# Cached attention of a two-layer hybrid decoder: queries on rows, three column groups, a product scan, and one chain of four-page units over all samples

## What is computed

```python
def stick_breaking(q, k, v, q_pos, k_pos):
    z = jnp.einsum('bqhd,bkhd->bhqk', q, k).astype(jnp.float32) * HEAD_DIM ** -0.5
    causal = (k_pos[None, :] < q_pos[:, None])[None, None]
    log_beta = jax.nn.log_sigmoid(z)
    log_keep = jnp.where(causal, jax.nn.log_sigmoid(-z), 0.0)
    after = lax.cumsum(log_keep, axis=3, reverse=True) - log_keep
    a = jnp.where(causal, jnp.exp(log_beta + after), 0.0)
    return jnp.einsum('bhqk,bkhd->bqhd', a.astype(v.dtype), v)

    logits = jnp.einsum('bqgrd,bqkgd->bqgrk', qg, kg).astype(jnp.float32) * HEAD_DIM ** -0.5
    logits = jnp.where(valid[:, :, None, None, :], logits, -jnp.inf)
    p = jax.nn.softmax(logits, axis=-1)
    o = jnp.einsum('bqgrk,bqkgd->bqgrd', p.astype(v.dtype), vg)
```

## Time and profile before

| | |
|---|---|
| median of 3 runs | 5645.08 us (5630.95 to 5647.56) |
| profiled execution | 5633.87 us, span 5632.3 us |
| samples' attention, layer 0 | 2113 to 2583 us of the span |
| samples' attention, layer 1 | 4908 to 5385 us |
| granted PE clock, mean of the span | 0.933 |

### The profile page before, as it was taken

One profiled execution on the slowest core, in us unless ns is written; L12 is line 12 of the kernel. 1 busy time (PEld: TensorE's weight loads), 2 busy tenths in 40 slices (PEclk: granted clock), 3 DMA queues, 4 the chain that ended last, 5 costly groups with the idle time before them and its releaser, 6 DMA issues.

```text
span 5632.3 us, 72888 instructions
## 1 busy us (share of the span) xinstructions
...
## 2 busy tenths in 40 slices
...
GB/s 61 32 9 51 58 21 53 53 61 98 60 46 22 18 69 133 183 138 144 106 38 30 11 58 48 21 59 62 50 105 48 48 20 24 90 145 151 168 97 89
DMA packets 344766, 390.79 MB, mean 69 GB/s; under 512 B 102775, under 2 KB 266706, under 8 KB 340978
## 3 DMA queue, kind: packets, MB, share of 16 engines
...
## 4 chain that ended last, share of the span: by engine, by line
PE 78%; DVE 7%; issue 5%; ACT 4%; SPq 2%; POOL 1%; DMA 1%; ACTq 1%; POOLq 0%; DVEq 0%
PE banks L801 17%; PE banks L804 13%; PE banks L1748 8%; PE banks L312 5%; PE banks L1509 4%; PE banks L1077 4%; PE banks L1109 4%; PE banks L1094 4%; DVE arena L402 3%; PE banks L1534 3%; PE banks L1501 3%; PE banks L1292 3%; PE banks L1307 2%; PE banks L1282 2%; ACT arena L1321 1%
## 5 line engine op out<-in xcount | busy, mean ns | idle before, releaser
L903 DVE TENSOR_SCALAR_CACHE_REDUCE arena<-arena 128x384 uint8<-128x384 f32 (+14 forms) x960 | 1405.1, 1533 | 7.2 <-DVE arena L941 0.9
L801 PE MATMUL banks<-arena 128*128 128x512 f32 x2176 | 937.4, 592 | 0.0
L804 PE MATMUL banks<-arena 128*128 128x384 f32 (+3 forms) x2336 | 720.3, 464 | 3.0 <-POOLq L147 3.0
L801 PEld LDWEIGHTS banks<-arena 128*128 128x128 f32 x2176 | 409.9, 189 | 523.2 <-issue 523.2
L1193 DVE TENSOR_TENSOR_SCAN arena<-arena 128x129 f32<-128x129 f32 (+3 forms) x480 | 525.7, 1139 | 142.5 <-ACT arena L1121 121.6
L1337 POOL TENSOR_SCALAR arena<-arena 128x128 f32<-128x128 f32 (+15 forms) x192 | 577.8, 3021 | 138.4 <-DVE arena L1367 138.4
L804 PEld LDWEIGHTS banks<-arena 128*128 128x128 f32 (+1 forms) x2336 | 417.5, 182 | 269.3 <-issue 62.9
L1748 PE MATMUL banks<-arena 128*128 128x512 f32 (+1 forms) x1088 | 471.3, 596 | 13.0 <-SPq L147 13.0
L1356 DVE CUSTOM_DVE_ANT_0 arena<-banks,arena 128x512 f32<-128x512 f32 (+3 forms) x480 | 274.1, 608 | 333.8 <-PE banks L1282 313.4
L336 PE MATMUL banks<-arena 64*128 64x512 f32 (+3 forms) x1216 | 321.0, 627 | 136.8 <-ACT arena L384 134.5
L402 DVE SCALAR_TENSOR_TENSOR arena<-arena 128x512 f32<-128x512 f32 (+3 forms) x532 | 393.1, 739 | 56.3 <-ACT arena L384 0.7
...
## 6 DMA issues: line engine op xcount, KB each, us to landing
arena<-in_cache_sb_kv SPq DMA_DIRECT2D x256, 384.0 KB
arena<-in_cache_dsa_kv SPq DMA_DIRECT2D x256, 128.0 KB
...
```

Source lines behind the costliest of these rows:

```text
L801: m = nc.tensor.matmul(bank[i % 4][:, :], W2[c % 2][:, k, j * P:(j + 1) * P], xT[:, k, t * FREE:(t + 1) * FREE], start=(k == 0), stop=(k = ...
L804: m = nc.tensor.matmul(bank[i % 4][0:rows_of(t), 0:WD[name]], xT[:, k, t * P:t * P + rows_of(t)], W2[c % 2][:, k, 0:WD[name]], start=(k == ...
L903: nc.vector.tensor_scalar(out[0:r, 0:v.shape[-1]], v, thr[0:r, t:t + 1], 0.0, ALU.is_ge, ALU.add, accum_out=cnt[0:r, t:t + 1]).then_inc(s_ ...
```

## The change

`sattn_*` is written anew. The logits of both mixers now stand with queries on partitions and keys in columns. The work of all 8 samples is one straight chain of 40 **units**, five to a sample: the 8 new keys (c = 0), then four chunks of four pages, last pages first. Page buffers are per chunk (8 for stick, 10 for sparse). In step s of the chain PE does `logits(s-1)`, `keys(s)`, `weights(s-3)` and `values(s-4)`.

- Per unit the stick logits are three matmuls of 512 columns, one for each head pair, whose outputs lie at partitions 0, 32 and 64 of one bank (32, 32 and 16 query rows); the sparse logits are one of 48 rows.
- ACT takes the sigmoid of minus z, DVE a product scan from the last key backwards, carried from unit to unit, POOL the difference of neighbours, which is the weight. Exp, Ln, softplus, the 16-step sum and the constant matrices are gone.
- PE transposes the weights (80 rows stick, 48 rows sparse, the sparse ones five units later, after the softmax of the whole sample), DVE copies both to SBUF, PE applies the values in the same three column groups.
- ACT loads the sigmoid table before the stage and changes to the Exp table and back once per sample. It also issues half of the sparse page loads.
- The bias is stored as one row per sample, head and query (384 rows, 48 DMAs at the start of the stick stage where there were 8) and loaded by two DMAs per sample. Query rows of all samples are loaded once. Results are stored once, by 12 DMAs after the chain, and waited for at t = 2 of the output stage.
- Small set-up constants change (`negtri`, `negones`, `newmask`, `newbias` go, `octets`, `notcausal` come).

The diff, cut to what the steps speak of:

```diff
-    SBD = nc.dram_tensor("sample_bias", (NS, NKEY), F32).ap()
+    SBD = nc.dram_tensor("sample_bias", (NB * HDSA * NQ, NKEY), F32).ap()
...
-                sp.dma_start(SBD[b * NQ:(b + 1) * NQ, :], scs[a:a + 2 * NQ - 1:2, :]).then_inc(s_bs, 16)
+                for h in range(HDSA):
+                    r = (b * HDSA + h) * NQ
+                    sp.dma_start(SBD[r:r + NQ, :], scs[a:a + 2 * NQ - 1:2, :]).then_inc(s_bs, 16)
...
+                    sp.wait_ge(s_az0, at(s_az0, l + 1))
+                    load_queries(sp, l)
+                    load_first_pages(sp, l)
...
+            nc.gpsimd.memset(alg_1[:, 0:2 * NB * P], 0.0).then_inc(s_az0, 1)
...
+        ACH, APC, NAU = 5, 4, 5 * NB
+        SROWS, DROWS, CW4 = 80, HDSA * NQ, APC * P
+        NAV = NAU + ACH
...
+        QROWS = (32, 32, 16)
...
+        def chunk(n):
+
+            b, c = unit(n)
+            return 4 * b + c - 1
...
+        def keys_at(c):
+
+            return (NPG * P, NKEY) if c == 0 else ((4 - c) * CW4, (5 - c) * CW4)
...
+        def page(queue, q, jj):
+            b, j = q // 4, (3 - q % 4) * APC + jj
+            return queue.value_load(pages[0:1, b * NPG + j:b * NPG + j + 1], min_val=0, max_val=N_POOL - 1)
+
+        def load_stick_page(queue, l, q, jj, pg):
+            queue.dma_start(asb[q % NASB][:, jj, :], sb_pool[l, ds(pg, 1), :, :].rearrange("o p c -> (o p) c")).then_inc(s_apg[q % NASB], 16)
+
+        def load_sparse_page(queue, l, q, jj, pg):
+            queue.dma_start(ada[q % NADA][:, jj, :], dsa_pool[l, ds(pg, 1), :, :].rearrange("o p c -> (o p) c")).then_inc(s_apg[q % NASB], 16)
...
         def sattn_sync(sp, l):
...
+            U0, V0 = l * NAU, l * NAV
+            for n in range(-2, NAU):
+                if n + 2 < NAU and (n + 2) % ACH and chunk(n + 2) >= 4:
+                    q = chunk(n + 2)
+                    if q >= NASB:
+                        sp.wait_ge(s_aav, at(s_aav, V0 + chunk_unit(q - NASB) + 1))
+                    for jj in range(APC):
+                        pg = page(sp, q, jj)
+                        load_stick_page(sp, l, q, jj, pg)
+                        if jj < 2:
+                            if jj == 0 and q >= NADA:
+                                sp.wait_ge(s_aav, at(s_aav, V0 + chunk_unit(q - NADA) + ACH + 1))
+                            load_sparse_page(sp, l, q, jj, pg)
+                if n >= 0 and n % ACH in (0, 2):
+                    b, half = n // ACH, n % ACH // 2
+                    if b:
+                        sp.wait_ge(s_abd, at(s_abd, U0 + (b - 1) * ACH + (3, 5)[half]))
+                    load_bias(sp, b, half)
+            sp.wait_ge(s_aav, at(s_aav, V0 + chunk_unit(24) + ACH + 1))
...
+            sp.wait_ge(s_aye, at(s_aye, 2 * NB * (l + 1)))
+            for h in range(HSB):
+                store_y(sp, h)
...
         def sattn_gpsimd(pool, l):
...
+                    pool.wait_ge(s_asc, at(s_asc, U0 + n + 1))
+                    if c:
+                        pool.wait_ge(s_awf, at(s_awf, V0 + max(0, n - 1)))
+                        nc.gpsimd.tensor_tensor(awv[u][0:SROWS, :], astay[u][0:SROWS, 1:FREE + 1], astay[u][0:SROWS, 0:FREE],
+                                                ALU.subtract).then_inc(s_adf, 1)
...
         def sattn_tensor(pe, l):
...
+            def logits(n):
...
+                        pe.wait_ge(s_ake[v], at(s_ake[v], C0 + chunk(n) + 1))
+                pe.wait_ge(s_akeep, at(s_akeep, U0 + n))
+                for p in range(4):
+                    kT = akT[:, p * CW4:(p + 1) * CW4] if c else akTn[:, p * NS + b * NQ:p * NS + (b + 1) * NQ]
+                    if p < 3:
+                        r = slice(32 * p, 32 * p + QROWS[p])
+                        k = nc.tensor.matmul(bank[4][r, 0:w], aqT[:, b, r], kT, start=True, stop=True)
+                        if p == 2:
+                            k.then_inc(s_azs, 1)
+                    else:
...
+                        nc.tensor.matmul(bank[5][0:DROWS, 0:w], adqT[:, b, :], kT, start=True, stop=True).then_inc(s_azd, 1)
...
+            def keys(n):
+                q = chunk(n)
+                pe.wait_ge(s_apg[q % NASB], at(s_apg[q % NASB], page_loads(l, q)))
+                for p in range(4):
+                    for jj in range(APC):
+                        src = asb[q % NASB][:, jj, p * P:(p + 1) * P] if p < 3 else ada[q % NADA][:, jj, 0:P]
+                        k = nc.tensor.transpose(bank[p][:, jj * P:(jj + 1) * P], src, ident[:])
+                    if p % 2:
+                        k.then_inc(s_akf[p // 2], 1)
...
+            def weights(m):
+                pe.wait_ge(s_awe, at(s_awe, V0 + m))
...
+                    pe.wait_ge(s_adf, at(s_adf, weights_ready(l, m) + 1))
+                    if c:
+                        for jj in range(APC):
+                            k = nc.tensor.transpose(bank[6][:, jj * SROWS:(jj + 1) * SROWS], awv[m % 2][0:SROWS, jj * P:(jj + 1) * P], ident[0:SROWS, 0:SROWS])
...
+                    r, c = unit(m - ACH)
...
+                    if c:
+                        pe.wait_ge(s_aex, at(s_aex, l * NB + r + 1))
+                        for jj in range(APC):
+                            e = keys_at(c)[0] + jj * P
+                            k = nc.tensor.transpose(bank[6][:, a + jj * DROWS:a + (jj + 1) * DROWS], alg[r % 2][0:DROWS, e:e + P], ident[0:DROWS, 0:DROWS])
...
+                k.then_inc(s_awf, 1)
...
+            def values(m):
+                pe.wait_ge(s_awe, at(s_awe, V0 + m + 1))
...
+                    for jj in range(APC if c else 1):
+                        for p in range(3):
+                            r = slice(32 * p, 32 * p + QROWS[p])
+                            a = jj * SROWS + 32 * p
+                            rows = slice(0, P if c else NS)
+                            v = asb[chunk(m) % NASB][:, jj, 384 + p * P:384 + (p + 1) * P] if c else anew[:, 384 + p * P:384 + (p + 1) * P]
+                            k = nc.tensor.matmul(bank[7][r, 0:P], awp[m % 2][rows, a:a + QROWS[p]], v,
+                                                 start=(c == 0), stop=(c == ACH - 1 and jj == APC - 1), skip_group_check=True)
...
+                    b, c = unit(m - ACH)
+                    for jj in range(APC if c else 1):
+                        a = APC * SROWS + jj * DROWS
+                        rows = slice(0, P if c else NS)
+                        v = ada[chunk(m - ACH) % NADA][:, jj, P:2 * P] if c else anew[:, 896:1024]
+                        k = nc.tensor.matmul(bank[7][0:DROWS, P:2 * P], awp[m % 2][rows, a:a + DROWS], v,
+                                             start=(c == 0 and m >= NAU), stop=(c == ACH - 1 and jj == APC - 1), skip_group_check=True)
+                k.then_inc(s_aav, 1)
+
...
+            for s in range(1, NAV + 4):
+                if s - 1 < NAU:
+                    logits(s - 1)
+                if s < NAU and s % ACH:
+                    keys(s)
+                if 0 <= s - 3 < NAV:
+                    weights(s - 3)
+                if 0 <= s - 4 < NAV:
+                    values(s - 4)
...
         def sattn_scalar(act, l):
...
+            for s in range(1, NAU + 2):
...
+                if n < NAU:
+                    w = CW4 if n % ACH else NQ
+                    act.wait_ge(s_azs, at(s_azs, U0 + n + 1))
+                    act.wait_ge(s_asc, at(s_asc, U0 + max(0, n - 1)))
+                    nc.scalar.activation(akeep[n % 2][0:SROWS, FREE - w:FREE], bank[4][0:SROWS, 0:w], ACT.Sigmoid, scale=-1.0).then_inc(s_akeep, 1)
+                if s < NAU and s % ACH:
+                    q = chunk(s)
+                    act.wait_ge(s_akf[0], at(s_akf[0], C0 + q + 1))
+                    act.wait_ge(s_azs, at(s_azs, U0 + s))
+                    nc.scalar.copy(akT[:, 0:2 * CW4], psum[:, 0:2 * FREE]).then_inc(s_ake[0], 1)
+                if s + 2 < NAU and (s + 2) % ACH and chunk(s + 2) >= 4:
+                    q = chunk(s + 2)
+                    if q >= NADA:
+                        act.wait_ge(s_aav, at(s_aav, V0 + chunk_unit(q - NADA) + ACH + 1))
...
+                if s % ACH == 0:
+                    r = s // ACH - 1
+                    load_functions(act, EXP_LN_SET)
+                    act.wait_ge(s_amx, at(s_amx, 3 * (l * NB + r) + 2))
+                    nc.scalar.activation(alg[r % 2][0:DROWS, :], alg[r % 2][0:DROWS, :], ACT.Exp, bias=anm[r % 2][0:DROWS],
+                                         accum_out=ars[r % 2][0:DROWS]).then_inc(s_aex, 1)
+                    if r < NB - 1:
+                        load_functions(act, SIGMOID_SET)
...
         def sattn_vector(dve, l):
...
+                    dve.wait_ge(s_azd, at(s_azd, U0 + n + 1))
+                    dve.wait_ge(s_ab[c // 3], at(s_ab[c // 3], 16 * (l * NB + b + 1)))
...
+                    nc.vector.tensor_tensor_reduce(alg[b % 2][0:DROWS, a:e], bank[5][0:DROWS, 0:w], abias[0:DROWS, a:e], 1.0, OUT_OF_REACH,
```

(18 more changed lines are left out.)

471 lines of the change are left out of this document (202 added, 269 removed).

## The result

The changed kernel takes 5223.3 us, the median of four runs (5219.7 to 5227.5); the kernel before took 5639.7 beside it (5631.0 to 5647.6). The ratio is 0.9262, with a 95% interval of 0.9244 to 0.9281. The forecast was 5220. A second comparison on another chip gave 5220.3, ratio 0.9259 (0.9232 to 0.9285). The profiled execution took 5226.7 us.

A forecast was written before the change was run, and what follows sets the result against it. PE, fed in a bad order, not bandwidth, bounds the kernel; two attention layers at 263 us replace 947, saving 421: 5634 - 421 = 5213, called 5220 us for run spread. Forecast case 5170 to 5265; 5150 to 5350 holds 0.81.

The forecast's parts named there:

- Unit price 6.5: PE time per full attention unit: logits 1.9, keys 1.8, weights 0.8, values 2.0 us; 32 units per layer.
- Three groups: Stick logits and values: matmuls in three column groups share the time of one, 0.86 us each.
- the rival: Attention units: column groups take turns at full clock, 9.8 us a unit, 106 us more a layer, 5430 us; chance 0.09.
- the 0.1s of the sum: Small additions of 0.1 us to the unit's keys and values, taken to include the array's mode changes.
- DVE's loop: Logits, bias, maximum, scan and key copy before the next logits: 5.6 us, hidden but barely under PE's 6.5.
- ScalarE's 6.8 us per sample: Sample end: page loads, table loads and exponential in one piece make the next key copy 1 us late, 7 us a layer.
- Page loads: Attention stage: 7.1 to 8.0 us per 2.2 MB chunk, 28 chunks in 199 to 223 us, nearly even with PE.
- Clock: Granted clock of 0.95 over the attention stage, costing 12 us a layer.
- The argument from the prompt's sparse stage: Clock stays high in attention, since the prompt's sparse stage is a third transposes too and has 0.99.
- rivals 1 and 3: Attention clock: swings as before (about 0.78), 5320 us, chance 0.20 with its like; or stays at 1.2 GHz, 5575, chance 0.05.
- Stores and weights at the end, 5 + 5 + 2: Attention stage's end, per layer: chain drain 5 us, result stores 5, exposed output weights 2.
- Elsewhere: nothing: Outside attention: 40 more bias stores hold SP 28 us early in the stick stage, costing nothing because loads are needed later.

The follow-up runs named there:

- one_group: Changed kernel, but the three stick head-pair matmuls, for logits and values, run one after another in one place instead of three column groups: 5428.4 us, ratio 0.9635.
- scan_twice: Changed kernel plus a second product scan of the same size per unit on VectorE, into an unread tile, before the real one: 5263.3 us, ratio 0.9345.
- half_pages: Changed kernel, but from the ninth chunk on only the key half of each stick page is loaded: 5212.6 us, ratio 0.9255.
- no_tables: Changed kernel with a sigmoid in place of the sparse exponential and without the two table loads around it: 5226.3 us, ratio 0.9279.

## Why the prediction was right

- **What bounds.** Right. PE's work in a feed that doesn't stop: PE is busy for 228 of 259 us, and for 138.4 of 143.4 us in the steady stretch.
- **Unit price 6.5.** Right, part by part, and 6.54 from logits to logits. But the forecast counted a sample as four such units, a short one of 1.3 and 1 us of delay, 28.3; the sample took 27.7 where no page was late, which leaves 1.5 for the short unit and nothing for a delay, and 28.4 to 28.7 with late pages.
- **Three groups.** Right: 0.98 and 1.00, and one_group prices the rival at 205 us, where 210 were forecast. That the array changes its mode about six times per unit is inside these prices. The Trainium skill, "TensorEngine Tiling (Array Packing)", Key Properties, says that each change drains the engine; nothing beyond the 0.1s of the sum shows.
- **DVE's loop.** Right, 5.3. I wrote 5.6, but the terms that I named (2.1, 0.78, 1.3 and 1.2) add up to 5.4. "Hidden, but barely" is what scan_twice shows.
- **ScalarE's 6.8 us per sample.** Wrong place. I had the first key copy late by 1 us seven times a layer. In half_pages, with the table loads in, every steady sample but one is 27.7, so nothing is late there. The table loads cost PE 1.1 to 2.8 us once, in a layer's first two samples, and no_tables shows no gain from it as long as the pages are whole.
- **Page loads.** Right: a share of 0.97 at 308 GB/s, and PE waits for them by up to 1.7 us where layer 0's steady samples begin. This, and not ScalarE, is the delay at the border.
- **Clock.** I took 0.95 over the stage, 12 us. The mean was 0.96, but not spread out: in layer 0 it was 1.00 but for 13.7 us at the start and 9.6 at the end, when PE had nothing to do, and in layer 1 low for 6.8 us at the start, 3.4 in the second sample and 11 at the end. So it cost less than 12. The argument from the prompt's sparse stage was the good one; rivals 1 and 3 did not happen. The Trainium skill, "TensorE: Matmul & The Clock Gate", Part 4, says that transposes do not count as PE work for the clock; 2.55 us of the unit's 6.54 are transposes, and the granted clock stayed at 1.00.
- **Stores and weights at the end, 5 + 5 + 2.** The terms fell short: from the last value matmul to the output stage it takes 12.1 and 13.9, where 5 for the stores and 2 for the weights were forecast; the drain lies before it. The step "the output weights are now asked for some 19 us before the stage ends" looked only at when the weights land. It missed that the requests themselves stand ahead of the stores on the same queue.
- **"Elsewhere: nothing".** This step failed. The 28 us on SyncE were counted about right (31.5 for all 48 stores, where eight had taken 5.7), but I looked at who needs the loads behind them, not at the result stores behind those loads. The stick stages lost 9.5 us in this pair of profiles. Another 12 came with the later rise of the clock, which I had not thought of, and which no run ties to the change.

Sum of the misses: 9 us too much in the stages, 24 too little elsewhere. That the time was hit so closely is luck: they are of opposite sign.
